# One row in four of the expert sum moved from TensorE to ScalarE and GpSimd, and the front of the work order rearranged

## Chip, cores, metric

The kernel runs on one core of a Trainium2 chip. The metric is the device time of one execution in microseconds, the median of several runs. One execution is recorded by the hardware profiler; its span and the rows below come from that one.

## What is computed

Two layers over 256 tokens of width 1024, in float32. Each layer has a mixing part and an expert part. The mixing part (RMS norm, one input projection, three kinds of attention, an S5 state space model, one output projection) is added to x. The expert part takes 128 expert rows for each token out of a table of 16384 and adds their weighted sum:

```python
q = (xc @ wq).reshape(c, PEER_HEADS, 2, PEER_QDIM // 2)
sc = jnp.einsum('thpd,hpkd->thpk', q, keys)
top_v, top_i = lax.top_k(sc, PEER_TOPK)
...
best_v, best_pos = lax.top_k(cand, PEER_TOPK)
ids = jnp.take_along_axis(cand_id, best_pos, axis=-1)
gate = jax.nn.softmax(best_v, axis=-1)
act = jax.nn.gelu(jnp.einsum('td,thkd->thk', xc, u_tab[ids])) * gate
return jnp.einsum('thk,thkd->td', act, v_tab[ids])   # added to x
```

## The kernel before

Tokens stand on the 128 partitions, so the 256 tokens are two blocks, and two layers of two blocks make four passes (PASSES, numbered 0 to 3). In each pass a token has 128 slots (SLOTS, 8 heads of 16 experts). For one slot, GpSimd issues one indirect DMA that gathers for each partition the u row and the v row of its expert, 8 KB together, 1 MB in all, into one of ten places of `ring` (RING, `ring_u` and `ring_v`). So a pass has 128 gathers and the kernel 512.

Slots are worked in groups of four (RING_G); a pass has 32 such turns (HALVES), and a turn's number in a pass is i, over the whole kernel m = 32 n + i. In a turn VectorE makes four dot products of u rows with the normed tokens (`take_dots`; the product is written back over the u row, the sum goes to `dots`), ScalarE takes their gelu (`acts`), VectorE multiplies by the gates (`weights`), and ScalarE scales the identity by each weight (`weigh`, giving `diag`). TensorE multiplies each diagonal with the v row, two halves of 512 columns, and accumulates over all 128 slots of the pass in two PSUM banks (`add_rows`, L1578). Each finished row raises `v_used`, on which GpSimd waits before it gathers into that place again, ten gathers later. At the end of a pass VectorE adds the two banks to x (`gathered`). In the last pass the tokens for the dot products are kept in PSUM, in the other passes in SBUF (`h`).

While pass n gathers, the mixing part and the search of pass n + 1 are done in between. `plan_steps` writes out one order of named steps, and each engine walks through that list and does its share of every step; inside an engine the order is fixed, between engines semaphores decide. In the list a turn is: "dots", "weigh", the search steps ("best", "pairs", "ids") and the mixing steps given to that turn, and then "rows of v". The last two turns of the last pass are done slot by slot. The mixing of pass 0 has nothing to hide behind; its order is the list `first`. The steps of it that the change touches:

- "steps 0": ScalarE's exponent of the S5 time step (L539), which waits for the load of the S5 parameters. "rows 0": TensorE transposes the tokens, VectorE and ScalarE (L599) copy four columns of blocks each into `hT`, which the projection ("columns", L1321) needs.
- "tables 0": VectorE turns sines into the S5 tables (L810 to L852); TensorE transposes its blocks in "turned 0" (L1294). "z 0": VectorE (L921) and ScalarE copy the projection out of PSUM.
- "turn back" and "turn on": VectorE's rotations before and after the S5 scan. "turn on 1" raises `s5_state`, for which TensorE's step "y 0" waits.

SyncE's queue issues all weight loads; it isn't touched. The GpSimd queue holds the gathers in order of slots.

## Time and profile before

| | us |
|---|---|
| median of 3 runs | 1610.1 |
| lowest and highest | 1606.73, 1611.24 |
| the profiled execution | 1609.26 |
| its span | 1607.4 |

The span is what the profile covers; the time of an execution has 1.9 us more around it. PE is TensorE, PEld its weight loads, DVE is VectorE, ACT ScalarE, POOL GpSimd. Each row of a group of instructions names line, engine, operation, output and inputs, and the count behind x. For TensorE one float32 multiplication shows as two instructions, so a row of v (two halves) is four. The clock that TensorE was granted stands as a share of 2.4 GHz.

### The profile page before, as it was taken

Reading aid. Unit: us, or ns where it says so; the run is one execution under the profiler, and the core shown is the slowest. Engines: PE = TensorE matmul, PEld = TensorE weight load, DVE = VectorE, ACT = ScalarE, POOL = GpSimd, SP = SyncE. Lnnn points to the kernel's source line nnn. Section 1 sums busy time; section 2 is a strip of 40 time slices with the busy share of each in tenths; the row PEclk is TensorE's granted clock in tenths of the full one; section 3 lists DMA queues with packets and bytes.
Section 4 is the critical chain, followed back from the end, with each engine's and each line's share of the span. In section 5 each row is a group of like instructions: output and inputs, shape, how many; then the busy total and the mean of one; then the engine's idle time right before and its main releaser. Section 6 shows DMA issues by size and latency. Waiting matters only on the chain.

```text
span 1607.4 us, 15416 instructions
## 1 busy us (share of the span) xinstructions
PE 1420.3 (88%) x4754; PEld 767.6 (48%) x4754; DVE 1130.7 (70%) x2797; ACT 464.6 (29%) x1127; POOL 588.5 (37%) x525
## 2 busy tenths in 40 slices
PE   6898879999998898897998799899998888877778
PEld 3667435554464344454465344555456533333333
DVE  5838998867667797785457788787556796765555
ACT  3432234342322224333121233334222222121112
POOL 1003325554323343453433434355341433434332
PEclk9999989999999999999999999999999998989999
DMA  9449999999999999999999999999999999999997
GB/s 361 153 175 381 388 377 378 402 393 420 416 412 421 410 422 363 419 420 419 421 414 402 423 422 420 421 399 396 420 418 407 374 406 423 421 421 421 421 421 328
DMA packets 103134, 632.09 MB, mean 393 GB/s; under 512 B 9697, under 2 KB 10977, under 8 KB 35214
## 3 DMA queue, kind: packets, MB, share of 16 engines
q0 software_dynamic: 74144, 537.97, 81.4%
q1 hardware_dynamic: 28910, 93.14, 14.9%
q8 instruction: 39, 0.64, 0.2%
q14 instruction: 41, 0.34, 0.1%
HBM read 630.01 MB, written 1.06 MB: 393 GB/s over the span
## 4 chain that ended last, share of the span: by engine, by line
PE 52%; DMA 20%; DVE 17%; issue 6%; ACT 3%; another core or an unknown queue 1%; POOL 0%; SPq 0%; POOLq 0%; DVEq 0%; ACTq 0%
PE ps L1578 30%; DMA ring<-table_uv,ids 20%; PE ps L1545 7%; DVE ring L1218 6%; PE ps L1358 3%; PE ps L1523 3%; PE ps L1321 2%; ACT acts L730 1%; ACT diag L753 1%; PE ps L1425 1%; PE ps L1561 1%; DVE W L996 1%; DVE W L1191 1%; DVE W L1193 1%
## 5 line engine op out<-in xcount | busy, mean ns | idle before, releaser
L1578 PE MATMUL ps<-ring,diag 128*128 128x512 f32 x2016 | 939.7, 622 | 142.7 <-ACT diag L753 129.4
L1630 POOL DMA_INDIRECT ring<-table_uv,ids x512 | 583.2, 1139 | 981.2 <-PE ps L1578 844.7
L1578 PEld LDWEIGHTS ps<-ring,diag 128*128 128x128 f32 x2016 | 394.3, 200 | 636.9 <-issue 620.4
L1218 DVE CUSTOM_DVE_ANT_0 ring<-ring,h 128x1024 f32<-128x1024 f32 x384 | 456.6, 1223 | 163.1 <-DMA ring<-table_uv,ids 160.8
L730 ACT ACTIVATE acts<-dots,small 128x4 f32<-128x4 f32 x126 | 37.4, 297 | 849.2 <-DVE dots L1218 819.8
L1218 DVE CUSTOM_DVE_ANT_0 ring<-ring,ps 128x1024 f32<-128x1024 f32 x120 | 144.7, 1220 | 95.1 <-DMA ring<-table_uv,ids 94.8
L753 ACT ACTIVATE diag<-cst,weights 128x128 f32<-128x128 f32 x504 | 161.0, 390 | 29.0 <-DVE weights L1227 28.7
L1545 PE MATMUL ps<-hT,W 128*128 128x128 f32 x960 | 114.3, 282 | 12.6 <-DMA W<-peer_wq 12.6
L1545 PEld LDWEIGHTS ps<-hT,W 128*128 128x128 f32 x960 | 113.1, 198 | 16.4 <-issue 16.4
L1358 PE MATMUL ps<-W,hT 128*128 128x512 f32 (+2 forms) x256 | 95.2, 527 | 2.7 <-DVE hT L870 2.7
L1358 PEld LDWEIGHTS ps<-W,hT 128*128 128x128 f32 x256 | 48.6, 190 | 51.9 <-issue 47.3
L1227 DVE TENSOR_TENSOR weights<-acts,gates 128x4 f32<-128x4 f32 x126 | 20.6, 163 | 53.8 <-ACT acts L730 53.8
L1523 PE MATMUL ps<-W,hT 128*128 128x512 f32 x128 | 57.3, 594 | 0.8 <-DVE hT L1084 0.8
L730 ACT ACT_TABLE_LOAD x43 | 55.2, 1283 | 4.8 <-DVE dots L1218 4.0
L1218 DVE DVE_READ_ACCUMULATOR2_ANT dots<- 128x1 f32 x504 | 41.6, 82 | 0.0
L1523 PEld LDWEIGHTS ps<-W,hT 128*128 128x128 f32 x128 | 24.0, 190 | 29.2 <-issue 28.2
L709 ACT ACTIVATE W<-ps 128x512 f32<-128x512 f32 x15 | 9.0, 597 | 97.5 <-PE ps L1545 97.5
L1019 DVE TENSOR_REDUCE small<-ps 128x4 f32<-128x512 f32 (+1 forms) x16 | 15.3, 956 | 27.1 <-PE ps L1435 14.7
L1425 PE MATMUL ps<-W 128*128 128x256 f32 (+1 forms) x128 | 31.9, 331 | 1.7 <-ACT W L661 1.7
L661 ACT ACTIVATE W<-ps,small 128x128 f32<-128x128 f32 (+1 forms) x64 | 26.0, 418 | 22.9 <-DVE small L1020 22.8
L1425 PEld LDWEIGHTS ps<-W 128*128 128x128 f32 x128 | 21.4, 191 | 7.1 <-issue 6.3
L1435 PE MATMUL ps<-bias,cst 128*128 128x128 f32 (+1 forms) x96 | 23.6, 327 | 0.0
(291 smaller groups left out, 1149.0 us busy)
## 6 DMA issues: line engine op xcount, KB each, us to landing
W<-peer_wq SPq DMA_DIRECT2D x13, 2048.0 KB, 28.5
W<-w_in SPq DMA_DIRECT2D x16, 1282.0 KB, 10.5
W<-w_out SPq DMA_DIRECT2D x8, 2048.0 KB, 18.6
ring<-table_uv,ids POOLq DMA_INDIRECT x512, 12.9
W<-w_in SPq DMA_DIRECT2D x8, 898.0 KB, 8.4
W<-w_in SPq DMA_DIRECT2D x4, 1024.0 KB, 11.5
ring<-w_in SPq DMA_DIRECT2D x2, 1544.0 KB, 18.8
ring<-w_in SPq DMA_DIRECT2D x2, 1536.0 KB, 21.1
```

The costliest lines, as they stand in the source:

```text
L661: a.activation(pbuf[:, i, 0:nk], lg[:, i * nk:(i + 1) * nk], ACT.Exp, bias=small[:, 72 + i:73 + i], accum_out=small[:, 80 + i:81 + i]).the ...
L730: a.activation(acts[:, g * RING_G:(g + 1) * RING_G], dots[:, g * RING_G:(g + 1) * RING_G], ACT.Gelu_apprx_tanh, scale=ffn_rstd[n % NB]).th ...
L753: a.activation(diag[:, s, :], ident, ACT.Copy, scale=weights[:, s:s + 1]).then_inc(diag_ready, 1)
L1218: v.tensor_tensor_reduce(ring_u[:, r, :], ring_u[:, r, :], tokens, 1.0, 0.0, ALU.mult, ALU.add, dots[:, s:s + 1]).then_inc(dots_done, 1)
L1321: mm = pe.matmul(ps[:, z_bank(0, bank), 0:c1 - c0], hT[:, k, :], first_at[group][:, k, a0:a0 + c1 - c0], start=(k == 0), stop=(k == KC - 1))
L1358: mm = pe.matmul(ps[:, 2 + i, 0:c1 - c0], hT[:, k, :], win[:, slot, c0:c1], start=(k == 0), stop=(k == KC - 1))
L1425: pe.matmul(dst, q, k, start=True, stop=False)
L1435: mm = pe.matmul(dst, flip, bias[:, t, SEQ - nk:SEQ], start=False, stop=True)
L1523: mm = pe.matmul(ps[:, 2 + c, :], hT[:, k, :], half[:, k % 4, c * 512:(c + 1) * 512], start=(k == 0), stop=(k == KC - 1))
L1545: mm = pe.matmul(ps[:, 6 + q % 2, i * P:(i + 1) * P], wq_at(n, q)[:, k, i * P:(i + 1) * P], hT[:, k, :], start=(k == 0), stop=(k == KC - 1))
L1578: mm = pe.matmul(ps[:, c, :], diag[:, s, :], ring_v[:, r, c * 512:(c + 1) * 512], start=(k == 0), stop=(k == SLOTS - 1), skip_group_check= ...
L1630: gp.indirect_dma_start(ring[:, t % RING, :], None, table_uv, bass.IndirectOffsetOnAxis(ap=ids[:, b, k:k + 1], axis=0)).then_inc(pair_in[t ...
```

## The change

In turns 0 to 28 of every pass (`added(m)`), the fourth row of v isn't multiplied by a diagonal on TensorE. ScalarE, after the turn's three diagonals, scales the row in place in `ring_v` by its weight and raises `v_scaled`. GpSimd adds it to the 1024 columns of x of this block (`add_row`), right before it issues the gather into the same place, and waits for its own add. TensorE accumulates the other rows as before; `by_pe(m)` and `adds_by[m]` count the rows of each kind, and all waits on `diag_ready` and `v_used` follow them. VectorE's `gathered` waits for the pass's adds, and its `weigh` for the scaling of two turns earlier. 116 rows take the new way, 396 the old.

In the order of pass 0, "steps 0" stands ahead of "rows 0", "tables 0" ahead of the columns and "z 0", "turn back 1" right behind "turn back 0", and "turn on 0" and "turn on 1" one entry and two entries later.

```diff
+ADD_LAST = 28
...
-    first = [["rows 0", "steps 0", "lines", "square 0", "phases 0", "sines 0", "mean 0"],
-             ["columns 0", "columns 1", "columns 2", "columns 3", "z 0", "tables 0"],
+    first = [["steps 0", "rows 0", "lines", "square 0", "phases 0", "sines 0", "mean 0", "tables 0"],
+             ["columns 0", "columns 1", "columns 2", "columns 3", "z 0"],
...
-             ["keys 0", "columns 6", "columns 7", "turn back 0", "z 1", "next square"],
-             ["logits 0", "softmax 0", "next rows", "turn back 1"],
+             ["keys 0", "columns 6", "columns 7", "turn back 0", "turn back 1", "z 1", "next square"],
+             ["logits 0", "softmax 0", "next rows"],
...
-             ["columns 9", "heads 0", "columns 10", "keys 1", "columns 11", "differ 1", "z 2", "qk sums 3", "turn on 0"],
-             ["weights 1", "logits 4", "logits 5", "next columns 0", "next columns 1", "qk scale 1", "softmax 2", "turn on 1"],
+             ["columns 9", "heads 0", "columns 10", "keys 1", "columns 11", "differ 1", "z 2", "qk sums 3"],
+             ["weights 1", "logits 4", "logits 5", "next columns 0", "next columns 1", "qk scale 1", "softmax 2", "turn on 0"],
...
-             ["heads 2", "logits 6", "co sums"],
+             ["heads 2", "turn on 1", "logits 6", "co sums"],
...
+        def added(m):
+            return m % HALVES <= ADD_LAST
...
+        def by_pe(m):
+            return RING_G * m - adds_by[m]
...
+        def own_slots(m):
+            return RING_G - added(m)
...
# ScalarE, weigh
                 if m >= 2:
-                    a.wait_ge(v_used, RING_G * (m - 1))
-                for s in range(g * RING_G, (g + 1) * RING_G):
+                    a.wait_ge(v_used, by_pe(m - 1))
+                for s in range(g * RING_G, g * RING_G + own_slots(m)):
                     a.activation(diag[:, s, :], ident, ACT.Copy, scale=weights[:, s:s + 1]).then_inc(diag_ready, 1)
+                if added(m):
+                    t = RING_G * m + RING_G - 1
+                    s, r = t % HELD, t % RING
+                    a.wait_ge(pair_in[r], 16 * (t // RING + 1))
+                    a.activation(ring_v[:, r, :], ring_v[:, r, :], ACT.Copy, scale=weights[:, s:s + 1]).then_inc(v_scaled, 1)
...
# VectorE, weigh and gathered
                 if m >= 2:
-                    v.wait_ge(diag_ready, RING_G * (m - 1))
+                    v.wait_ge(diag_ready, by_pe(m - 1))
+                    v.wait_ge(v_scaled, adds_by[m - 1])
...
             def gathered(n, i):
                 b = n % NB
+                v.wait_ge(x_added, adds_by[HALVES * (n + 1)])
...
# TensorE, add_rows
-                for j in range(RING_G):
+                for j in range(own_slots(m)):
...
-                    pe.wait_ge(diag_ready, RING_G * m + j + 1)
+                    pe.wait_ge(diag_ready, by_pe(m) + j + 1)
...
# GpSimd
+            def add_row(m):
+                t = RING_G * m + RING_G - 1
+                r, b = t % RING, m // HALVES % NB
+                gp.wait_ge(v_scaled, adds_by[m + 1])
+                if adds_by[m]:
+                    gp.wait_ge(x_added, adds_by[m])
+                gp.tensor_tensor(x[:, b, :], x[:, b, :], ring_v[:, r, :], ALU.add).then_inc(x_added, 1)
+                gp.wait_ge(x_added, adds_by[m + 1])
...
                         if t >= RING:
-                            gp.wait_ge(v_used, t - RING + 1)
+                            m, j = (t - RING) // RING_G, (t - RING) % RING_G
+                            if j < own_slots(m):
+                                gp.wait_ge(v_used, by_pe(m) + j + 1)
+                            else:
+                                add_row(m)
```

## Rows read from the trace of the kernel before

**Rows 1.** Busy time of each engine, the page

```profile
PE 1420.3 (88%) x4754; PEld 767.6 (48%) x4754; DVE 1130.7 (70%) x2797; ACT 464.6 (29%) x1127; POOL 588.5 (37%) x525
```

**Rows 2.** The costliest groups of instructions, the page

```profile
L1578 PE MATMUL ps<-ring,diag 128*128 128x512 f32 x2016 | 939.7, 622 | 142.7 <-ACT diag L753 129.4
L1630 POOL DMA_INDIRECT ring<-table_uv,ids x512 | 583.2, 1139 | 981.2 <-PE ps L1578 844.7
...
L1218 DVE CUSTOM_DVE_ANT_0 ring<-ring,h 128x1024 f32<-128x1024 f32 x384 | 456.6, 1223 | 163.1 <-DMA ring<-table_uv,ids 160.8
...
L753 ACT ACTIVATE diag<-cst,weights 128x128 f32<-128x128 f32 x504 | 161.0, 390 | 29.0 <-DVE weights L1227 28.7
```

**Rows 3.** Windows by stage: busy of each engine, PE clock, DMA share, GB/s

```profile
160.00:260.00 100.00, 85.64 (x222) 41.15 (x223) 94.06 (x268) 32.79 (x72) 34.49 (x29) 0.91 0.94 372
...
310.00:340.00 30.00, 28.44 (x105) 16.48 (x104) 24.63 (x42) 13.31 (x33) 15.38 (x11) 1.00 0.95 372
...
550.00:620.00 70.00, 69.35 (x182) 33.57 (x181) 64.63 (x171) 26.11 (x54) 27.16 (x21) 1.00 0.95 384
...
1080.00:1100.00 20.00, 18.44 (x76) 11.24 (x75) 18.63 (x33) 9.52 (x21) 10.98 (x8) 1.00 0.94 349
...
1240.00:1280.00 40.00, 39.04 (x175) 24.30 (x174) 28.03 (x90) 8.69 (x20) 15.24 (x15) 1.00 0.94 365
1280.00:1320.00 40.00, 30.63 (x63) 12.63 (x62) 37.56 (x108) 10.10 (x24) 15.47 (x16) 0.91 1.00 408
1320.00:1580.00 260.00, 205.48 (x420) 85.10 (x419) 154.26 (x310) 46.70 (x136) 98.09 (x106) 0.91 1.01 421
```

**Rows 4.** POOL's issues by source: 900 to 1260 us, then 1340 to 1580

```profile
L1630 POOL DMA_INDIRECT ring<-table_uv,ids x123: 932/942/2009, 899.7 to 1258.6; - x123
...
DMA to landing us min/median/max: 5.5/12.9/21.0
...
L1630 POOL DMA_INDIRECT ring<-table_uv,ids x95: 932/936/1287, 1346.4 to 1579.9; - x95
```

**Rows 5.** Timeline of POOL: start, duration, instruction, idle before it

```profile
226.56 0.94 POOL L1630 DMA_INDIRECT ring<-table_uv,ids  x1 [1.01 <-PE ps L1578]
...
240.98 1.87 POOL L1630 DMA_INDIRECT ring<-table_uv,ids  x1 [12.10 <-PE ps L1578]
...
245.46 0.94 POOL L1630 DMA_INDIRECT ring<-table_uv,ids  x1 [0.30 <-issue]
...
255.62 0.94 POOL L1630 DMA_INDIRECT ring<-table_uv,ids  x1 [0.47 <-PE ps L1578]
```

**Rows 6.** Timeline of DVE in the same stretch

```profile
228.82 0.19 DVE L1195 SCALAR_TENSOR_TENSOR W<-W 128x32 f32<-128x32 f32 x1
...
240.89 1.16 DVE L1218 CUSTOM_DVE_ANT_0 ring<-ring,h 128x1024 f32<-128x1024 f32 x1
...
246.41 0.42 DVE L969 TENSOR_TENSOR h<-h,small 128x256 f32<-128x256 f32 x1
...
256.96 1.22 DVE L987 TENSOR_TENSOR W<-s5t,ps 128x1024 f32<-128x1024 f32 x1
```

**Rows 7.** A square of 1024 columns on ACT, ns min/median/max

```profile
L573 ACT ACTIVATE h<-x x4: 1039/1060/1072, 12.4 to 928.8; 128x1024 f32<-128x1024 f32 x4
```

**Rows 8.** Timeline of all engines at the front

```profile
8.21 1.28 ACT L599 ACT_TABLE_LOAD   x1 [8.21 <-PE ps L1280]
...
9.51 1.14 ACT L599 ACTIVATE hT<-ps,cst 128x128 f32<-128x128 f32 x4
...
11.79 0.21 ACT L539 ACTIVATE small<-W 128x8 f32<-128x8 f32 x1 [1.15 <-DMA W<-s_in]
...
21.86 1.06 ACT L553 ACTIVATE s5t<-W 128x1024 f32<-128x1024 f32 x1
...
27.00 0.75 DVE L921 TENSOR_SCALAR h<-ps,small 128x512 f32<-128x512 f32 x1 [6.01 <-PE ps L1321]
...
36.50 1.12 PE L1294 MATMUL ps<-cst,W 128*128 128x128 f32 x4 [5.94 <-DVE W L852]
```

More of the change, by code:

```diff
@@ L345, in trunk @@
             sem("dots_done"), sem("gelu_done"), sem("weights_done"), sem("diag_ready"), sem("v_used"))
-        x_done, low_done, x_low = sem("x_done"), sem("low_done"), sem("x_low")
+        x_done, low_done, x_low, x_added = sem("x_done"), sem("low_done"), sem("x_low"), sem("x_added")
+        v_scaled = sem("v_scaled")
         dve_step, act_step = sem("dve_step"), sem("act_step")
@@ L413, in searched @@
             return {4: 1, 5: 2, 1: 3, 2: 4, 3: 5}[i] if n == 0 else 4 * n + i + 2
+        def added(m):
+            return m % HALVES <= ADD_LAST
+        adds_by = [0]
+        for m in range(HALVES * PASSES):
+            adds_by.append(adds_by[-1] + added(m))
+        def by_pe(m):
+            return RING_G * m - adds_by[m]
+        def own_slots(m):
+            return RING_G - added(m)
         def parts_done(m):
@@ L741, in weigh_one @@
                 a.wait_ge(weights_done, parts_done(m - 1) + k % RING_G + 1)
-                a.wait_ge(v_used, SLOTS * n + k + 1 - HELD)
+                a.wait_ge(v_used, by_pe(m - 2) + k % RING_G + 1)
                 a.activation(diag[:, s, :], ident, ACT.Copy, scale=weights[:, s:s + 1]).then_inc(diag_ready, 1)
@@ L1239, in weigh_one @@
                 v.wait_ge(gelu_done, parts_done(m - 1) + k % RING_G + 1)
-                v.wait_ge(diag_ready, SLOTS * n + k + 1 - HELD)
+                v.wait_ge(diag_ready, by_pe(m - 2) + k % RING_G + 1)
                 v.tensor_tensor(weights[:, s:s + 1], acts[:, s:s + 1], gates[:, n % NB, k:k + 1], ALU.mult).then_inc(weights_done, 1)
@@ L1247, in gathered @@
                     v.tensor_tensor(x[:, b, 0:512], x[:, b, 0:512], ps[:, 0, :], ALU.add).then_inc(x_low, 1)
-                    v.wait_ge(v_used, SLOTS * (n + 1))
+                    v.wait_ge(v_used, by_pe(HALVES * (n + 1)))
                     v.tensor_tensor(x[:, b, 512:D], x[:, b, 512:D], ps[:, 1, :], ALU.add).then_inc(x_done, 1)
                     return
-                v.wait_ge(v_used, SLOTS * (n + 1))
+                v.wait_ge(v_used, by_pe(HALVES * (n + 1)))
                 v.tensor_tensor(x[:, b, :], x[:, b, :], ps[:, 0:2, :].rearrange("p c n -> p (c n)"), ALU.add).then_inc(x_done, 1)
@@ L1586, in add_row @@
                 pe.wait_ge(pair_in[r], 16 * (t // RING + 1))
-                pe.wait_ge(diag_ready, t + 1)
+                pe.wait_ge(diag_ready, by_pe(t // RING_G) + k % RING_G + 1)
                 for c in range(2):
```

## The prediction

> **What bounds the kernel now.** I read the page's busy shares first [rows 1]: PE 88%, DVE 70%, POOL 37%, ACT 29%. PE looks like the bound, and the change takes work from PE. But the windows by stage [rows 3] say otherwise. From 1320 to 1580 us, where only gathered rows are consumed, the DMA engines move 421 GB/s with a share of 1.01, while PE is busy 205 of 260 us. That is the ceiling, and a gather of 1 MB (128 rows of 8 KB) costs 2.5 us of it (1.05/421). Long stretches elsewhere stand at the same rate, so relief of PE is worth something only in stretches below it. What each lost against 421 GB/s is its length times (1 - rate/421):
>
> - 160 to 260 us: 372 GB/s, 11.6 us lost, DVE 94% busy, PE 86%.
> - 310 to 340: 372, 3.5 us lost, DVE 82%, PE 95%.
> - 550 to 620: 384, 6.2 us lost, DVE 92%, PE 99%.
> - 1080 to 1100: 349, 3.4 us lost, DVE 93%, PE 92%.
> - 1240 to 1280: 365, 5.3 us lost, DVE 70%, PE 98%.
> - 1280 to 1320: 408, 1.2 us lost, DVE 94%, PE 77%.
>
> So four stretches wait at least partly for PE, 18.4 us together, and two wait for DVE, the engine that does the top-k search and the dot products. The landing time of a gather (median 12.9 us [rows 4]) against 2.5 us each says that some five are outstanding: a slot that comes free a few us late costs nothing where the rate is 421.
>
> **What the change does to PE.** A row of v costs PE 939.7/504 = 1.86 us [rows 2]. Turns 0 to 28 of four passes are 116 rows: 116 x 1.86 = 216 us of PE time go, 1.86 us per turn. Busy 1420 becomes about 1204 (75%). By the table this is cover elsewhere; it can give back at most the 18.4 us.
>
> **ScalarE.** A diagonal of 0.39 us [rows 2] becomes a scaling of 1024 columns, 1.06 us by the square of the same shape [rows 7]: +0.67 us x 116 = 78 us on an engine 29% busy. It stands after the three diagonals that PE wants, so PE's rows don't wait for it; ScalarE's next step does, by 0.67 us, which the DVE work hides (if that cover were gone: 116 x 0.67 = 78 us spread over the turns; I keep 0). It is finished 3 x 0.39 + 1.06 = 2.2 us after the weights, sooner than PE frees its third row.
>
> **GpSimd.** The trace has no POOL arithmetic. The nearest rows: DVE does a two-input pass of 128x1024 in 1.22 us [rows 2], so below 1.2 us is not to be expected; twice that, 2.4 us, is the upper bound I use (two operands read in turn). I take 2.4, the dearer end, because in this trace POOL is the engine that is slowed beside DVE: its issue of a gather takes 0.94 us at the median but up to 2.01 us where the dot products read two operands from SBUF, and at most 1.29 us in the last pass, where one operand comes from PSUM [rows 4]. POOL: 588 + 116 x 2.4 = 867 us, 54% of the span. Behind each add stand, in POOL's queue, the gather that reuses this slot and all later ones. Per turn that is 4 x 1.14 + 2.4 + about 0.2 for the wait on the add's own semaphore = 7.2 us, under the 10.1 us that DMA needs for four gathers: 0 where five are outstanding. The cover is the queue of outstanding gathers [rows 4]; if only one gather were outstanding, each turn would cost the 2.6 us.
>
> **What the add does to DVE.** This decides. Two-operand DVE passes hold up POOL's issue: the one at 240.98 took 1.87 us beside the dot products from 240.89 on, the one at 245.46, as they ended, 0.94 us [rows 5, 6]. The add reads two SBUF operands itself and is longer, so the hold can go the other way too. I lay it behind the third gather of a turn, in four turns of the trace, and ask what DVE wants then [rows 5, 6]. Where dot products are running as it comes, as at 240.89, it gets in between two of them and holds 2.4 us. After 226.56+0.94 = 227.5: the pass then running ends at 228.1, the add lasts to 230.5, and the two-input step of 228.82 waits 1.7 us. After 245.46+0.94 = 246.4: one scaling of 0.42 us is under way, then the next is held about 2.0 us. After 255.62+0.94 = 256.6: DVE reads PSUM until 259.3, nothing is held. Mean 1.5 us per add; bounds 0 (no hold) and 2.4 (always the whole).
>
> On holds the Trainium skill ("SBUF — State Buffer", section "Who interferes with whom") says that a DVE instruction with two SBUF inputs and a GpSimd one that reads SBUF exclude each other, the later one waiting for the whole of the earlier; that would put this term toward the rival of full holds below, and the stretched issues of [rows 4, 5] agree in direction. The Trainium skill ("GPSIMD Engine Reference", section 3.1) gives 4497 ns for an add of 2048 columns; half, 2.25 us, is an estimate by that page and would make the hold 1.4 us instead of 1.5.
>
> Now stage by stage. 160 to 260 us: about 7 turns with an add, 7 x 1.5 = 10.5 us; DVE is idle 5.9 us there, of which I let 1.5 absorb: +9. 550 to 620: 5 turns, 7.5 us, against 5.4 us of DVE idle: +2, and PE's 5 x 1.86 = 9.3 us buys nothing since DVE becomes the bound. 1280 to 1320: dot products read PSUM, only the search contends: +1. 1240 to 1280: DVE has room, PE saves 1.86 us in each of three or four turns: -4 of the 5.3. 310 to 340 and 1080 to 1100: DVE 82% and 93%, so PE's relief is shared with DVE's holds: -2.5 of the 6.9. Elsewhere DMA is at or near its ceiling: 0.
>
> **The front.** Two moves of consequence. First, ScalarE's exponent for the S5 state now stands before its four copies of hT. Its input landed just before 11.79 us, after the copies of before were done (table load at 8.21, copies from 9.51 for 1.14 us) [rows 8]. So table load, exponent and copies follow one another from 11.8: 1.28 + 0.21 + 1.14, and PE's first columns start at about 14.5 instead of right behind 10.65: +3.8 us. Second, the S5 tables on DVE now stand before the evacuation of z, which waited for PE until 27.00. The tables followed it, and PE, which needs them for the transposes of the blocks, stood idle 5.94 us until 36.50 [rows 8]. From 27.75 (27.00 + 0.75) that is 8.7 us of tables. They now begin when the sines are there, which was 21.86 + 1.06 = 22.9 before and is some 1.2 us later behind the moved table load, about 24.1, and end about 32.8. The evacuation follows until 33.5, the transposes of the blocks are no longer stalled behind the tables, and PE reaches the next columns about 3 us sooner in spite of its late start. The S5 rotation ("turn on"), some 8 us of DVE, and half of "turn back" only change place; the rotation now ends later against its reader (y), so part of the 3 us is lost again. Between 0 and -3, with the first bound +3.8 if the late start is not hidden: I take -1.5. SP's queue issues nothing more and nothing later. The other waits added are free: on the scaling of two turns before, and, at a pass's end, on adds that stand in POOL's queue before the last three gathers of that pass.
>
> **Sum.** +9 +2 +1 -4 -2.5 -1.5 = +4 us on the profiled execution of 1609.26 us (span 1607.4): 1613 us. The median of the runs shown is 1610.1, so that is +0.2%. 0.3% (4.8 us) is about what a measurement of this kernel can tell from no change.
>
> **Rivals.**
> - *The adds don't hold DVE* (chance 0.34). For it: no DVE row in the trace is stretched by POOL, the dot products stay at 1.22 us; against it: POOL's instructions there are short and read hardly anything. Then the DVE-bound stretches cost 0, PE's relief recovers about 12 of 18.4 us: 1609.3 - 12 - 1.5 = 1596 us.
> - *Every add holds DVE whole* (0.24). 7 x 2.4 = 17 us in 160 to 260, 5 x 2.4 - 5.4 = 7 in 550 to 620, 3 in 1280 to 1320, only 4 recovered and 1.5 at the front: +22, 1631 us. For it: from the stretched issues, whoever comes second waits. It decides from a mean hold of about 2 us; below 1.3 the whole is no slower than before.
> - *The front's late start isn't hidden* (0.06): 3.8 instead of -1.5, 1618 us. Against it speaks PE's idle 5.94 us.
> - *Forecast* (0.36), its own range 1604 to 1621: faster 0.05, same 0.21, slower 0.10.
>
> Faster: 0.34 + 0.05 = 0.39. Same: 0.21 + 0.01 from the front's rival = 0.22. Slower: 0.10 + 0.24 + 0.05 = 0.39. The range 1592 to 1631 takes in the two main rivals' values and leaves out the first's far end and the second's.
>
> **What would show it.** PE busy near 1200 us; ScalarE +78 us. The POOL add: 2.4 us, if nearer 1.3 the hold shrinks and I am too high. DVE passes with two SBUF inputs stretched to 2 to 3.6 us or gaps before them, in passes 0 to 2, none in the last pass. 160 to 260: fewer than 372 GB/s, the search ending 9 us later; the 365 GB/s at 1240 gone. PE's first columns at 14.5 us and the first gather 1.5 us earlier. Wrong would be: DVE untouched beside the adds, a rate at 550 to 620 near 421, or gathers in the 421 GB/s stretches landing so late that the rate drops there, which would make it far slower than the range.

## The result, and the profile after

The changed kernel takes 1659.8 us in the median of 4 runs (1658.65 to 1660.16), the kernel before beside it 1610.7 us. The ratio is 1.0317, with an interval of 1.0304 to 1.0331: 49 us slower, outside the predicted range and above the dearest rival (1631).

The page of the kernel after: its span, the busy time of each engine, and the engines' shares of the chain that ended last.

```profile
span 1658.4 us, 14608 instructions
...
PE 1294.9 (78%) x4290; PEld 704.1 (42%) x4290; DVE 1331.9 (80%) x2797; ACT 549.3 (33%) x1127; POOL 876.9 (53%) x641
...
DVE 40%; PE 25%; DMA 17%; issue 9%; ACT 5%; POOL 3%; another core or an unknown queue 1%; SPq 0%; DVEq 0%; POOLq 0%; ACTq 0%
```

PE has lost 125 us and is at 78%. DVE has gained 201 us with the same 2797 instructions as before: 1331.9 against 1130.7 [rows 1]. DVE is now first in the chain with 40%. In the kernel before it was PE:

```profile
PE 52%; DMA 20%; DVE 17%; issue 6%; ACT 3%; another core or an unknown queue 1%; POOL 0%; SPq 0%; POOLq 0%; DVEq 0%; ACTq 0%
```

The costliest groups (busy us, mean ns of one, idle before it and what ended it):

```profile
L1603 PE MATMUL ps<-ring,diag 128*128 128x512 f32 x1552 | 808.6, 678 | 302.8 <-ACT diag L771 292.9
...
L1241 DVE CUSTOM_DVE_ANT_0 ring<-ring,h 128x1024 f32<-128x1024 f32 x384 | 510.5, 1371 | 88.0 <-DMA ring<-table_uv,ids 85.8
...
L1634 POOL TENSOR_TENSOR x<-x,ring 128x1024 f32<-128x1024 f32 x116 | 277.2, 2390 | 2.4
...
L1251 DVE TENSOR_TENSOR weights<-acts,gates 128x4 f32<-128x4 f32 x126 | 144.3, 1145 | 54.7 <-ACT acts L748 54.7
```

The same small product in the kernel before:

```profile
L1227 DVE TENSOR_TENSOR weights<-acts,gates 128x4 f32<-128x4 f32 x126 | 20.6, 163 | 53.8 <-ACT acts L730 53.8
```

The add lasts 2.39 us. The dot products went from 1223 to 1371 ns [rows 2], 54 us in all. The last row is the larger find: the product of gelu values and gates, 128x4 elements, went from 0.163 to 1.145 us at the mean. That is 126 x 0.98 = 124 us, more than half of what DVE gained, in an instruction that had only 20.6 us before. In the trace 56 of the 126 products are long, and each of these ends within 0.05 us after an add.

Stages of [rows 3] in the kernel after (busy us of PE, PEld, DVE, ACT, POOL; PE clock, DMA share, GB/s). The same times hold somewhat earlier work here, since everything is late by 10 to 55 us.

```profile
160.00:260.00 100.00, 70.94 (x170) 33.38 (x170) 94.26 (x247) 32.79 (x60) 40.83 (x30) 0.81 0.83 322
310.00:340.00 30.00, 26.71 (x114) 17.67 (x112) 28.96 (x41) 12.84 (x31) 21.38 (x15) 0.98 0.95 353
550.00:620.00 70.00, 56.30 (x138) 26.76 (x137) 60.86 (x141) 21.05 (x39) 30.83 (x23) 0.90 0.96 398
...
1240.00:1280.00 40.00, 32.03 (x180) 23.07 (x180) 28.51 (x74) 14.35 (x30) 24.81 (x17) 0.97 1.02 413
...
1320.00:1580.00 260.00, 173.44 (x314) 71.07 (x315) 190.63 (x406) 68.46 (x140) 152.87 (x125) 0.82 1.01 414
```

160 to 260 us moves 322 GB/s instead of 372, with DVE as full as before: the same engine does less for its time. In the last pass DVE rises from 154 to 191 us and the rate is 414, not 421. Two stretches that ran at the ceiling before, before and after:

```profile
620.00:740.00 120.00, 103.89 (x364) 56.64 (x363) 88.78 (x179) 45.67 (x120) 53.74 (x46) 0.96 1.02 418
1100.00:1240.00 140.00, 131.17 (x487) 75.38 (x486) 80.34 (x193) 35.02 (x91) 55.42 (x48) 0.96 1.02 417
```

```profile
620.00:740.00 120.00, 84.43 (x270) 44.63 (x269) 113.35 (x195) 50.61 (x111) 73.44 (x50) 0.88 0.96 381
1100.00:1240.00 140.00, 120.32 (x384) 64.68 (x382) 110.58 (x163) 54.69 (x114) 97.95 (x64) 0.92 0.97 388
```

DVE goes there from 74% to 94% and from 57% to 79%, and the rate falls to 381 and 388. The page's median time from a gather's issue to its landing falls from 12.9 to 10.3 us: with gathers also issued at a slower pace, fewer of them are outstanding at a time.

The best measure of where it was lost is the time at which GpSimd issues gather number k, taken from its timeline in each kernel (us; each column after the first is the difference from before):

| gather | before | after | adds only in turns 0 to 19 | adds only in turns 20 to 28 | row scaled, not added | VectorE multiplies and adds |
|---|---|---|---|---|---|---|
| 0 | 124.0 | -2.8 | +1.9 | -1.6 | +2.1 | -2.8 |
| 32 | 226.6 | +9.8 | +21.3 | +3.3 | +6.5 | +9.5 |
| 80 | 359.6 | +20.6 | +34.1 | +5.3 | +1.0 | +7.0 |
| 160 | 614.6 | +22.5 | +34.1 | +2.5 | -1.5 | +9.9 |
| 208 | 740.5 | +38.7 | +50.2 | +2.6 | +5.0 | +13.4 |
| 256 | 893.5 | +31.3 | +49.7 | -1.0 | +0.3 | +7.9 |
| 336 | 1124.4 | +49.4 | +61.4 | +2.0 | -2.7 | +9.5 |
| 384 | 1271.3 | +46.2 | +63.0 | -1.5 | -3.3 | +9.3 |
| 464 | 1467.8 | +55.5 | +73.2 | +0.3 | +1.1 | +13.9 |
| 511 | 1586.4 | +52.6 | +69.6 | +3.8 | +1.1 | +13.5 |

A pass is 128 gathers. The kernel after loses in the first 80 gathers of each pass; behind them nothing more is lost in pass 0 and some comes back in the others: -2.8 at the first gather, then +12.6, +10.8, +1.9, +16.2, -7.4, +18.1, -3.2, +9.3, -2.9.

Each column is a single execution, so small differences say little. Three kernels that work as the kernel before does up to gather 32, but for the order of the front or the engine that makes the weights, also lose 4.8 us between gathers 0 and 32, so about 5 of the 12.6 us belong to the one trace of the kernel before. The column of turns 0 to 19 is the longest of that kernel's four runs (1678.8 us, median 1671.3).

**How a hold looks.** One turn of the first pass in the timeline of all engines (start, duration, instruction, idle before it):

```profile
171.35 1.97 POOL L1669 DMA_INDIRECT ring<-table_uv,ids  x1 [0.32 <-issue]
...
172.55 0.30 ACT L748 ACTIVATE acts<-dots,small 128x4 f32<-128x4 f32 x1 [7.54 <-DVE dots L1241]
172.88 2.84 DVE L1251 TENSOR_TENSOR weights<-acts,gates 128x4 f32<-128x4 f32 x1 [0.36 <-ACT acts L748]
173.34 2.34 POOL L1634 TENSOR_TENSOR x<-x,ring 128x1024 f32<-128x1024 f32 x1
...
175.75 0.98 ACT L771 ACTIVATE diag<-cst,weights 128x128 f32<-128x128 f32 x3 [2.90 <-DVE weights L1251]
176.30 7.99 PE L1603 MATMUL ps<-ring,diag 128*128 128x512 f32 x12 [5.73 <-ACT diag L771]
...
180.32 0.94 POOL L1669 DMA_INDIRECT ring<-table_uv,ids  x1 [3.42 <-PE ps L1603]
```

The product that should take 0.16 us is on DVE from 172.88 to 175.72. A gather's issue was under way as it came (until 173.32); the add follows at 173.34 and ends at 175.68, and only then does the product finish. ScalarE has idled 2.90 us for it, PE 5.73 us, and the gather that wants the first freed slot is issued at 180.32. The next two timelines show the other forms, a dot product in the second pass and the search in the last:

```profile
564.42 2.37 POOL L1634 TENSOR_TENSOR x<-x,ring 128x1024 f32<-128x1024 f32 x1
564.78 3.10 DVE L1241 CUSTOM_DVE_ANT_0 ring<-ring,h 128x1024 f32<-128x1024 f32 x1
...
567.81 1.21 DVE L1241 CUSTOM_DVE_ANT_0 ring<-ring,h 128x1024 f32<-128x1024 f32 x1
```

```profile
1442.19 3.47 DVE L1179 TENSOR_TENSOR W<-W 128x256 f32<-128x256 f32 x2
...
1443.01 2.36 POOL L1634 TENSOR_TENSOR x<-x,ring 128x1024 f32<-128x1024 f32 x1
...
1450.03 1.22 DVE L1241 CUSTOM_DVE_ANT_0 ring<-ring,ps 128x1024 f32<-128x1024 f32 x1
1450.33 2.36 POOL L1634 TENSOR_TENSOR x<-x,ring 128x1024 f32<-128x1024 f32 x1
```

At 564.78 a dot product comes 0.36 us behind the add and lasts 3.10 us, ending about 1.1 us after the add does; the next takes 1.21. In the last pass the two 128x256 products of the search, 0.41 us each elsewhere, last 3.47 us, while the dot product of 1450.03, whose second operand is in PSUM, keeps its 1.22 us although an add starts 0.3 us into it.

**The front.** The timeline of all engines:

```profile
11.72 0.21 ACT L557 ACTIVATE small<-W 128x8 f32<-128x8 f32 x1 [9.69 <-DMA W<-s_in]
11.83 1.12 ACT L617 ACTIVATE hT<-ps,cst 128x128 f32<-128x128 f32 x4
...
13.06 16.28 PE L1346 MATMUL ps<-W,hT 128*128 128x512 f32 x32 [4.11 <-ACT hT L617]
...
32.61 0.60 PE L1319 MATMUL ps<-cst,W 128*128 128x128 f32 x4
```

The exponent waited 9.69 us for its input, the copies followed at 11.83, and PE's first columns began at 13.06. The transposes of the blocks stand at 32.61 us, against 36.50 before [rows 8], and the next columns followed at 33.04, 4.4 us sooner than before (37.41), where about 3 had been forecast.

### The profile page after: what moved, and what is told of

The parts are those of the page before. It is cut to its first block, busy times and chain, and to the rows that moved or that the text cites. A ratio compares the mean times of both kernels' runs of the same rounds, so it can differ in the third digit from the quotient of the medians.

```text
span 1658.4 us, 14608 instructions
## 1 busy us (share of the span) xinstructions
PE 1294.9 (78%) x4290; PEld 704.1 (42%) x4290; DVE 1331.9 (80%) x2797; ACT 549.3 (33%) x1127; POOL 876.9 (53%) x641
## 4 chain that ended last, share of the span: by engine, by line
DVE 40%; PE 25%; DMA 17%; issue 9%; ACT 5%; POOL 3%; another core or an unknown queue 1%; SPq 0%; DVEq 0%; POOLq 0%; ACTq 0%
DMA ring<-table_uv,ids 15%; DVE ring L1241 14%; PE ps L1603 14%; DVE weights L1251 7%; PE ps L1570 6%; DMA W<-peer_wq 2%; POOL ring L1669 2%; ACT acts L748 1%; DVE W L1216 1%; DVE W L1214 1%; DVE W L1217 1%; PE ps L1548 1%; DVE W L1019 1%; POOL x L1634 1%
## 5 line engine op out<-in xcount | busy, mean ns | idle before, releaser
L1603 PE MATMUL ps<-ring,diag 128*128 128x512 f32 x1552 | 808.6, 678 | 302.8 <-ACT diag L771 292.9
L1669 POOL DMA_INDIRECT ring<-table_uv,ids x512 | 594.3, 1161 | 742.2 <-PE ps L1603 573.2
L1603 PEld LDWEIGHTS ps<-ring,diag 128*128 128x128 f32 x1552 | 329.8, 219 | 734.5 <-issue 721.6
L1241 DVE CUSTOM_DVE_ANT_0 ring<-ring,h 128x1024 f32<-128x1024 f32 x384 | 510.5, 1371 | 88.0 <-DMA ring<-table_uv,ids 85.8
L1634 POOL TENSOR_TENSOR x<-x,ring 128x1024 f32<-128x1024 f32 x116 | 277.2, 2390 | 2.4
L1251 DVE TENSOR_TENSOR weights<-acts,gates 128x4 f32<-128x4 f32 x126 | 144.3, 1145 | 54.7 <-ACT acts L748 54.7
L771 ACT ACTIVATE diag<-cst,weights 128x128 f32<-128x128 f32 x388 | 127.1, 391 | 152.7 <-DVE weights L1251 152.7
L776 ACT ACTIVATE ring<-ring,weights 128x1024 f32<-128x1024 f32 x116 | 131.4, 1133 | 0.0
L1216 DVE TENSOR_TENSOR W<-W 128x512 f32<-128x512 f32 (+1 forms) x34 | 26.9, 792 | 1.2
## 6 DMA issues: line engine op xcount, KB each, us to landing
ring<-table_uv,ids POOLq DMA_INDIRECT x512, 10.3
```

What stands on the lines that cost most here:

```text
L771: a.activation(diag[:, s, :], ident, ACT.Copy, scale=weights[:, s:s + 1]).then_inc(diag_ready, 1)
L776: a.activation(ring_v[:, r, :], ring_v[:, r, :], ACT.Copy, scale=weights[:, s:s + 1]).then_inc(v_scaled, 1)
L1216: step(v.tensor_tensor(hits, hits, bc(i4[:, :, s, :], 2, TOPK), ALU.mult))
L1241: v.tensor_tensor_reduce(ring_u[:, r, :], ring_u[:, r, :], tokens, 1.0, 0.0, ALU.mult, ALU.add, dots[:, s:s + 1]).then_inc(dots_done, 1)
L1251: v.tensor_tensor(weights[:, ss], acts[:, ss], gates[:, b, i * RING_G:(i + 1) * RING_G], ALU.mult)\
L1603: mm = pe.matmul(ps[:, c, :], diag[:, s, :], ring_v[:, r, c * 512:(c + 1) * 512], start=(k == 0), stop=(k == SLOTS - 1), skip_group_check= ...
```

## The experiments

**The two halves of the change.** One kernel has only the new order of the front:

```diff
-    first = [["rows 0", "steps 0", ... "mean 0"],
-             ["columns 0", ... "z 0", "tables 0"],
+    first = [["steps 0", "rows 0", ... "mean 0", "tables 0"],
+             ["columns 0", ... "z 0"],
```

> The kernel before with only the new order of the front. In the changed kernel the first gather was issued at 121.3 us instead of 124.0. Theory H (the adds hold VectorE) says the order is not what costs: first gather again near 121.3, time 2 to 3 us below before (0.998 to 0.999). The rival that the order does the harm (the S5 rotation too late for its reader, ScalarE late) wants a good part of the 49 us here: 1.01 or more.

1.0003 [0.9988, 1.0017]. Nothing that can be measured, where 2 to 3 us had been expected. Its first gather goes out at 125.6 us against 124.0; over the seventeen kernels profiled here that time scatters from 120.2 to 126.4, with either order, so the 4 us seen at 33 us cannot be found again at the gathers. The other kernel is the change with the old order:

> The changed kernel with the front order of before. Theory H: all of the loss stays and the front's gain goes, 1660 + 2.8 = about 1663 us (1.032 to 1.035 of before), first gather near 124. If the order and the adds do harm together: clearly under 1650.

1.0346 [1.0323, 1.0368], DVE busy 1335.6 us. The whole loss is the adds'.

**What the relief is worth by itself.** The row is neither multiplied nor added, so that its part of the sum is left out:

```diff
-                    a.activation(ring_v[:, r, :], ring_v[:, r, :], ACT.Copy, scale=weights[:, s:s + 1])
+                    a.activation(ring_v[:, r, 0:1], ring_v[:, r, 0:1], ACT.Copy, scale=weights[:, s:s + 1])
...
-                gp.tensor_tensor(x[:, b, :], x[:, b, :], ring_v[:, r, :], ALU.add).then_inc(x_added, 1)
```

> The fourth row of turns 0 to 28 is not used at all: no product on PE, no scaling (ScalarE scales a single column), no add; its gather and its dot product stay. This is the whole relief of PE with no cost beside it, left out of the sum. Theory H with the DMA ceiling: only the stretches below 421 GB/s that wait for PE come back, 8 to 18 us, plus 2.8 us of the front: 1590 to 1600. If PE were the bound of the kernel, up to 216 us of PE time would show in the end: under 1560.

0.9946 [0.9928, 0.9965]: 8.7 us, less than expected (1606.6 us, not 1590 to 1600). Its page:

```profile
PE 1288.1 (80%) x4290; PEld 704.0 (44%) x4290; DVE 1132.2 (71%) x2797; ACT 451.1 (28%) x1127; POOL 581.8 (36%) x525
```

PE is as relieved as in the kernel after (1288 against 1295 us), DVE is where it was before. So 116 of 512 rows taken from PE for nothing, nearly a quarter, bring half a per cent. With ScalarE's scaling of the whole row and still no add:

```diff
-                if adds_by[m]:
-                    gp.wait_ge(x_added, adds_by[m])
-                gp.tensor_tensor(x[:, b, :], x[:, b, :], ring_v[:, r, :], ALU.add).then_inc(x_added, 1)
-                gp.wait_ge(x_added, adds_by[m + 1])
```

> ScalarE scales the fourth row, GpSimd does nothing with it (left out of the sum) and only waits for the scaling. Between the run with the row left out (0.9946) and that with GpSimd's write of zeros (1.0002) this says whose the 9 us are: near 0.995 if the occupied GpSimd queue (1.8 us per add) cost them, near 1.000 if ScalarE's 1.13 us did. I expect the first, 0.995 to 0.998, since ScalarE's scaling stands behind the diagonals.

0.9956 [0.9940, 0.9971]. The 99 us of ScalarE time cost 0.0010, 1.6 us, which is within the uncertainty of the two ratios.

**Is it the reading of SBUF?** The add is replaced by a GpSimd instruction that only writes (the row is left out of the sum):

```diff
-                gp.tensor_tensor(x[:, b, :], x[:, b, :], ring_v[:, r, :], ALU.add).then_inc(x_added, 1)
+                gp.memset(ring[:, r, :], 0.0).then_inc(x_added, 1)
```

> GpSimd's add is replaced by a write of zeros over the same place of the ring, 2048 columns, which reads nothing from SBUF; the fourth rows of turns 0 to 28 are left out of the sum. GpSimd's queue is still occupied before the same gathers for about 1 to 2.4 us, ScalarE still scales, PE is relieved. Theory H (reads of the add exclude VectorE's passes with two SBUF inputs): VectorE's weights product back at 0.16 us from 1.15, dot products 1.22 from 1.37, time at or under before, 1595 to 1610. Rival Q (the add delays the gathers in GpSimd's queue): time stays near 1660 minus what the write is shorter, so 1640 or more.

1.0002 [0.9989, 1.0015], 1614 us, a little above the 1595 to 1610 expected and far from the rival's 1640. From the page of this kernel:

```profile
L1241 DVE CUSTOM_DVE_ANT_0 ring<-ring,h 128x1024 f32<-128x1024 f32 x384 | 457.8, 1226 | 198.2 <-DMA ring<-table_uv,ids 192.6
...
L1634 POOL MEMSET ring<- 128x2048 f32 x116 | 211.1, 1820 | 0.1
...
L1251 DVE TENSOR_TENSOR weights<-acts,gates 128x4 f32<-128x4 f32 x126 | 20.8, 165 | 48.4 <-ACT acts L748 47.7
```

116 writes of 1.82 us run beside DVE, and both DVE rows stand where they stood before: 1226 and 165 ns. These writes are 0.57 us shorter than the adds. With a second write of 640 columns behind the first:

```diff
+                gp.memset(ring[:, r, :], 0.0).then_inc(half_written, 1)
+                gp.wait_ge(half_written, adds_by[m + 1])
+                gp.memset(ring[:, r, 0:640], 0.0).then_inc(x_added, 1)
```

> As the run with GpSimd's write of zeros, lengthened by a second write of 640 columns to about 2.6 us with the wait between, a little longer than the add's 2.39; fourth rows left out of the sum. Reads nothing, holds nothing. Run with 1.82 us: 1.0002, without it 0.9956. If the queue's cost grows with the length: 1.002 to 1.006, so that the queue has some 10 of the 60 us between the changed kernel and the row left out. If the queue were the cause of the convex rest, 1.015 or more.

1.0019 [1.0005, 1.0033].

```profile
PE 1295.2 (80%) x4290; PEld 708.5 (44%) x4290; DVE 1160.7 (72%) x2797; ACT 549.6 (34%) x1127; POOL 869.0 (54%) x757
```

GpSimd is as busy as with the adds (869 against 877 us), DVE has gained 30 us and not 201. These 30 us are holds too, but of other instructions: mostly casts and scalings, which take one tensor. The cast of search results before, and in this kernel:

```profile
L1182 DVE CAST W<-W 128x64 f32<-128x64 uint32 x15 | 3.8, 252 | 0.0
```

```profile
L1205 DVE CAST W<-W 128x64 f32<-128x64 uint32 x15 | 10.1, 675 | 0.0
```

Against the kernel that scales and doesn't add, the writes cost 1.0019 - 0.9956 = 0.0063, some 10 us; each of the two has about 0.0015 of uncertainty on either side. How much of it is the occupied queue and how much these holds was not separated.

**Less reading.** One operand read, as a copy within the ring (row left out of the sum):

```diff
+                gp.tensor_copy(ring_u[:, r, :], ring_v[:, r, :]).then_inc(x_added, 1)
```

> GpSimd copies the scaled row onto the used u row (one SBUF operand read, 1024 columns) instead of adding it to x; the fourth rows of turns 0 to 28 are left out of the sum. Theory H (any read of GpSimd excludes VectorE's two-operand passes for the time of the whole GpSimd instruction): weights product and dot products are stretched again in proportion to the copy's duration; with a copy of about half the add's 2.39 us some 20 us of the 49 come back as loss, 1625 to 1640 on the scale of 1614 before. Rival (only GpSimd instructions with two operands contend): 1614 as with the write.

1.0026 [1.0013, 1.0039], 1619.5 us: below the 1625 to 1640 expected, and above the rival's 1614. Whether the copy holds VectorE is read from the rows:

```profile
L1634 POOL COPY ring<-ring 128x1024 f32<-128x1024 f32 x116 | 126.2, 1088 | 0.8
...
L1251 DVE TENSOR_TENSOR weights<-acts,gates 128x4 f32<-128x4 f32 x126 | 60.9, 483 | 48.8 <-ACT acts L748 48.4
```

And the add on half of the columns (the other half is left out):

```diff
+                gp.tensor_tensor(x[:, b, 0:512], x[:, b, 0:512], ring_v[:, r, 0:512], ALU.add).then_inc(x_added, 1)
```

> The add over 512 of the 1024 columns; the other half of the fourth rows is left out of the sum. Theory H, dose and response: add about 1.2 us, hold per add half (VectorE's extra busy time about 90 us instead of 201), and since the first holds are taken up by slack the loss falls by more than half: 1620 to 1632 on the scale of 1614 before. Rival Q (one more instruction in GpSimd's queue with its wait, whatever its length): 1645 or more.

1.0049 [1.0034, 1.0064], 1622 us. DVE gained 90 us (1220.8).

```profile
L1634 POOL TENSOR_TENSOR x<-x,ring 128x512 f32<-128x512 f32 x116 | 153.5, 1323 | 2.4
...
L1251 DVE TENSOR_TENSOR weights<-acts,gates 128x4 f32<-128x4 f32 x126 | 74.1, 588 | 48.5 <-ACT acts L748 48.5
```

The copy of 1.09 us holds the small product to 483 ns, the add of 1.32 us to 588, the add of 2.39 us to 1145, the write of 1.82 us to 165. One reading operand is enough to hold it, and the hold grows with the length of the instruction. The price grows faster than the hold: from the free relief it is 0.0103 for 90 us on DVE and 0.0371 for 201.

**Taking the small product off DVE.** ScalarE makes the weights, with the gates as its scale; and the same in the kernel before, as the control:

```diff
+                for j in range(RING_G):
+                    s, k = g * RING_G + j, RING_G * i + j
+                    w = a.activation(weights[:, s:s + 1], acts[:, s:s + 1], ACT.Copy, scale=gates[:, n % NB, k:k + 1])
+                w.then_inc(weights_done, 1)
```

> The changed kernel, but ScalarE makes the weights: four copies of acts with the gate as scale, in place of VectorE's product of acts and gates, the instruction that was stretched most (0.16 to 1.15 us, 124 of VectorE's extra 201 us). Theory H with the weights as the place that counts: the add runs beside instructions that matter less, 1625 to 1645 on the scale of 1614 before. If it doesn't matter which instruction is held because VectorE is full: the hold moves to the dot products and the time stays at 1655 or more.

> The kernel before with ScalarE making the weights, no adds: the control of the run above. It takes two crossings between engines and 0.16 us of VectorE out of each turn and adds about 0.8 us of ScalarE. With the DMA ceiling at 421 GB/s I expect no more than 5 us either way, 0.997 to 1.003.

1.0232 [1.0203, 1.0261] with the adds (1650 us, between the two expectations), 1.0037 [1.0023, 1.0051] without, just above the range expected. The page with the adds, and its dot products:

```profile
PE 1294.5 (79%) x4290; PEld 707.1 (43%) x4290; DVE 1250.9 (76%) x2671; ACT 656.8 (40%) x1631; POOL 880.6 (54%) x641
...
L1252 DVE CUSTOM_DVE_ANT_0 ring<-ring,h 128x1024 f32<-128x1024 f32 x384 | 525.7, 1407 | 138.9 <-DMA ring<-table_uv,ids 136.7
```

The adds now cost 1.0232 - 1.0037 = 0.0195 instead of 0.0317. So about 40% of the loss hung on the small product being on DVE. The rest moved to what DVE does instead: the dot products are at 1407 ns, and DVE is busy 140 us more than the control's 1111.

**Where in a pass.** The adds in turns 20 to 28 only (36 of them), and in 0 to 19 only (80):

```diff
-            return m % HALVES <= ADD_LAST
+            return 20 <= m % HALVES <= ADD_LAST
```

```diff
-ADD_LAST = 28
+ADD_LAST = 19
```

> Adds only in turns 20 to 28 of each pass, 36 adds, the turns that hold no mixing steps of the next pass but its queries and, early, nothing of the search of this one. By the issue times of the gathers the changed kernel lost nothing there. Theory H with a full VectorE as its condition: 0.997 to 1.002 of before. If each add costs the same wherever it stands (49/116 = 0.42 us): 36 x 0.42 = 15 us, 1.009.

> The other part: adds in turns 0 to 19, 80 adds. Theory H with its condition: the whole loss stays, 1.028 to 1.036. Same cost everywhere: 80 x 0.42 = 34 us, 1.021.

1.0000 [0.9986, 1.0014] and 1.0349 [1.0329, 1.0368].

```profile
PE 1376.3 (85%) x4610; PEld 750.3 (47%) x4610; DVE 1195.0 (74%) x2797; ACT 490.8 (30%) x1127; POOL 688.4 (43%) x561
```

```profile
PE 1350.7 (81%) x4434; PEld 733.8 (44%) x4434; DVE 1272.4 (76%) x2797; ACT 523.3 (31%) x1127; POOL 781.8 (47%) x605
```

DVE gains 64 us from 36 adds and 142 us from 80, 1.79 and 1.77 us per add: the hold is the same at both places, and its price is nothing at the one and the whole loss at the other. Turns 0 to 19 are where most of the next pass's mixing steps (normalization, S5) and the rest of the search stand between the dot products.

**The same work on DVE itself.** VectorE multiplies and adds in one instruction of 1.285 us, right behind the weights; ScalarE and GpSimd do nothing for it, and the sum is complete:

```diff
+                if added(m):
...
+                    v.scalar_tensor_tensor(out=x[:, b, :], in0=ring_v[:, r, :], scalar=weights[:, s:s + 1], in1=x[:, b, :],
+                                           op0=ALU.mult, op1=ALU.add).then_inc(x_added, 1)
```

> VectorE itself multiplies and adds the fourth row to x in one pass right behind the weights; ScalarE and GpSimd do nothing for it. The sum is complete. VectorE gets 116 x 1.22 = 142 us more of its own work, against 201 us of holds in the changed kernel, PE is relieved as there. If the end follows VectorE's busy time: between the half-width add (+90 us, 1.005) and the changed kernel (+201 us, 1.032), so 1.010 to 1.020. If what hurt was the place of the hold (the weights product, which all else in the turn waits for): below 1.008.

1.0045 [1.0027, 1.0063]. 141 us more on DVE (1272.1), as many as the 80 adds brought, for an eighth of their loss against the kernel before; counted from the free relief it is 0.0099, about a quarter of the 0.0371 of all 116 adds. Then with the long writes in GpSimd's queue as well:

> VectorE multiplies and adds (1.0045 alone), and GpSimd's queue is occupied by the same 2.6 us of writes before the gather. Sum complete. If the two costs simply add up: 1.0045 + 0.008 = 1.012. If VectorE's extra work and a later gather make each other worse, as they would have to in the changed kernel to explain its 1.032: 1.020 or more.

1.0134 [1.0110, 1.0158]: the writes cost 0.0089 here, against 0.0063 beside a less busy DVE. With 0.003 to 0.004 of uncertainty in the comparison the two are not told apart, so the costs add up as far as can be seen. And last, only the order is changed: the fourth weight alone, then the multiply-add, then the three weights that ScalarE and PE wait for:

```diff
+                    v.tensor_tensor(weights[:, s:s + 1], acts[:, s:s + 1], gates[:, b, k:k + 1], ALU.mult).then_inc(v_scaled, 1)
...
+                    v.scalar_tensor_tensor(out=x[:, b, :], in0=ring_v[:, r, :], scalar=weights[:, s:s + 1], in1=x[:, b, :],
+                                           op0=ALU.mult, op1=ALU.add).then_inc(x_added, 1)
+                    v.tensor_tensor(weights[:, s0:s0 + RING_G - 1], acts[:, s0:s0 + RING_G - 1], gates[:, b, k + 1 - RING_G:k],
+                                    ALU.mult).then_inc(weights_done, 1)
```

> VectorE makes the weight of the fourth row first, multiplies and adds that row (1.28 us), and only then makes the other three weights, on which ScalarE, PE and the freeing of the slots wait. Same work as in the run where the addition stands behind the weights (1.0045), plus 0.16 us a turn. Placement theory (a microsecond ahead of the weights is dear, behind them cheap): 1.012 to 1.025. If only VectorE's busy time counts: 1.005 to 1.008.

1.0120 [1.0097, 1.0143]. The timelines of the kernel with the multiply-add behind the weights, and ahead of them:

```profile
178.02 0.16 DVE L1245 TENSOR_TENSOR weights<-acts,gates 128x4 f32<-128x4 f32 x1 [0.36 <-ACT acts L748]
178.22 0.99 ACT L771 ACTIVATE diag<-cst,weights 128x128 f32<-128x128 f32 x3 [0.23 <-DVE weights L1245]
178.22 1.28 DVE L1253 SCALAR_TENSOR_TENSOR x<-ring,weights,x 128x1024 f32<-128x1024 f32 x1
...
178.76 8.27 PE L1605 MATMUL ps<-ring,diag 128*128 128x512 f32 x12 [4.77 <-ACT diag L771]
```

```profile
179.93 1.28 DVE L1253 SCALAR_TENSOR_TENSOR x<-ring,weights,x 128x1024 f32<-128x1024 f32 x1
181.13 0.16 DVE L1255 TENSOR_TENSOR weights<-acts,gates 128x3 f32<-128x3 f32 x1
...
181.32 0.99 ACT L771 ACTIVATE diag<-cst,weights 128x128 f32<-128x128 f32 x3 [1.62 <-DVE weights L1255]
...
181.86 7.70 PE L1610 MATMUL ps<-ring,diag 128*128 128x512 f32 x12 [5.37 <-ACT diag L771]
```

In the first, the diagonals start 0.20 us after the weights began and run beside the multiply-add. In the second they wait 1.4 us longer (1.62 against 0.23 us), and PE's rows start behind them. The same work, plus a second small product of 0.16 us a turn, costs 0.0075 (uncertain by 0.003), 12 us, more there: 0.10 us for each of 116 turns per 1.4 us of delay. That only some of the turns are short of time is the likely reason; no run shows which.

## Why the prediction was wrong

**The parts, as measured.** From the free relief (0.9946) to the kernel after (1.0317) are 0.0371, 60 us. ScalarE's scaling is 0.0010 of it and equally long writes in GpSimd's queue 0.0063, together 12 us. The remaining 0.030, 48 us, is there when GpSimd reads SBUF and gone when it only writes: two-operand work on DVE held by the adds. These are differences of ratios with about 0.002 of uncertainty each.

**What was right.** PE's relief as a thing of little worth (8.7 us by itself). The add at 2.4 us (2.39), which was the upper bound of a guess from a VectorE row, and GpSimd at 867 us (877). ScalarE +78 us (+85). The mean hold of 1.5 us was 0.2 short: 201/116 = 1.73; that is partly luck, since 62% of it fell on an instruction that the prediction did not look at. That dot products with an operand in PSUM go untouched; but "none in the last pass" was wrong, since search steps and 12 small products were held there. And the holds themselves: here the trace agrees with the Trainium skill ("SBUF — State Buffer", section "Who interferes with whom"), by which a DVE instruction with two SBUF inputs and a GpSimd one that reads SBUF exclude each other (dot products of 3.10 us beside the add, 1.22 us when one operand is in PSUM). The estimate by the Trainium skill ("GPSIMD Engine Reference", section 3.1), half of 4497 ns or 2.25 us, was 0.14 short of the measured 2.39.

**The step that failed: "Elsewhere DMA is at or near its ceiling: 0."** The forecast put a price on the holds of some 12 turns, and a shared one on a handful more, of the 116 with an add; that is why even its rival with 2.4 us for each add came only to 1631. Laid on the table of gathers, the stretches that I priced came out near their price. 160 to 260 us: +9 forecast, +12.6 by gather 32, some 5 of which are the scatter named above. 550 to 620: +2 forecast, +1.9 between gathers 80 and 160. 1240 to 1280: -4 forecast, -3.2 between 336 and 384. The stretches that I booked at nothing carry the loss: +10.8 between 32 and 80, +16.2 between 160 and 208, +18.1 between 256 and 336 (-2.5 was booked for a part of this and of the first together), +9.3 between 384 and 464 (about half of this, +4.5, also stands in the kernel with the row left out). The rates say the same: 381 instead of 418 GB/s from 620 to 740 us, 388 instead of 417 from 1100 to 1240. The ceiling of 421 GB/s was taken as a cover, as if a stretch near it had room for anything. A rate near the ceiling says that DMA is served in time by the engines as they are; it doesn't say how far they are from serving it late. With 1.73 us per turn on DVE and the rows' release behind it, they fell below. The prediction named this among what would make it wrong, and gave it no chance.

The +2 at 550 to 620 was luck. "PE's 5 x 1.86 = 9.3 us buys nothing since DVE becomes the bound" is not what the row left out shows: its rate there is 415 GB/s instead of 384, and it gains 5.9 us between gathers 128 and 160. The changed kernel loses 1.9 us there, so the holds cost near 8, where 7.5 had been counted and all but 2 written off against DVE's idle time; the relief covered the difference.

**The second step: a hold priced by its length alone.** I asked what DVE wants as the add comes, and counted dot products and search steps. The instruction that the add most often met was the weights product (56 of 116 adds): ScalarE's diagonals, PE's rows and the freeing of ring slots all stand behind it, so a hold there delays the turn itself and not only DVE's next step. It could have been seen in the trace of before: at the third gather's issue of 245.46 us [rows 5] that product follows at 245.86, and the prediction passed over it to the scaling of 246.41. The runs bear it out: without that product on DVE the adds cost 0.0195 instead of 0.0317, and DVE's own work of 141 us costs 0.010 over the free relief behind the weights and 0.017 ahead of them. In the turn shown the likely reason for the meeting is that the product comes at the end of the dot products, beside which the gather's issue ahead of the add was stretched to 1.97 us (171.35); in 33 of the 56 cases an issue was under way as the product came.

**The third: a queue cost of 0.** "0 where five are outstanding" was wrong by up to 10 us (0.0063), less what the holds of casts and scalings by the writes have of it. In the profiles the kernel with the long writes is 3.5 us ahead of the one without at the first gather (122.6 and 126.1 us), 8.0 behind at gather 80 (368.6 and 360.6) and 7.7 behind at the last (1595.2 and 1587.5). So in this pair of profiles the mean of 7.2 us per turn against 10.1 holds from then on, and the cost arises in the first 80 gathers, where in the kernel before the rate was 372 and GpSimd stood idle for PE, up to 12.10 us before a gather [rows 5]. That a gather there is not one of five outstanding that can wait is a reading, not shown by a run of its own.

**The clock was not it.** PE's matmuls went from 622 to 678 ns at a mean granted clock of 0.892 instead of 0.959, and 1204 x 0.959/0.892 = 1294 is what PE's busy time fell to (1295). But the kernel with the row left out has nearly the same (671 ns, clock 0.906) and is the fastest of all, so a clock at this level did not cost it its gain.

**The front.** The mechanism was there and earlier than forecast (columns at 13.06, not 14.5, since the table load was done while ScalarE waited), and it was worth nothing measurable instead of -1.5 us.

**What stays open.** The multiply-add ahead of the weights (0.0120), the writes in GpSimd's queue (0.0089) and the scaling (0.0010) add up to 0.022 of the 0.0317. The price rises faster than the hold (0.0103 for 90 us, 0.0371 for 201), the hold is 1.73 us against the multiply-add's 1.285, and it strikes other instructions too; whether that makes the remaining 0.010 was not separated. Nor is it settled why the adds in turns 0 to 19 alone (1.0349) cost no less than all 116 (1.0317, and 1.0346 with the old order). No version that computes the whole sum beat the kernel before: the nearest are the adds in turns 20 to 28 (1.0000) and VectorE's multiply-add (1.0045).

## What to carry to other kernels

Before work goes to GpSimd, list each VectorE instruction that reads two SBUF operands, the smallest too, and ask who waits for it: a 0.16 us product at the head of a chain costs more when it is held than a long one at its end. A stretch at the DMA ceiling is no cover by itself; it needs the slack of the chain that frees the buffers. And price the relief first: here a run with the row left out showed that all of it was worth half a per cent, less than VectorE's own multiply-add costs.

## What the runs showed of the hardware that was not expected

- A GpSimd instruction with a single SBUF operand (the copy, 1.09 us) holds VectorE's two-operand products as the add does (mean 483 ns instead of 163). One that only writes (1.82 us for 2048 columns) does not (165 ns).
- Writes hold other instructions of VectorE, with one tensor: beside the long writes the 128x64 casts took 675 ns at the mean instead of 252, and three scalings of only 128x4 took 1.78 to 2.18 us instead of 0.16, each with a write of 1.82 us under way before it ended. VectorE gained 30 us in all.
- A held instruction pays the whole wait whatever its size: a 128x4 product lasted up to 2.99 us, a dot product up to 4.05.
- A VectorE TENSOR_SCALAR of 128x128 with one SBUF tensor and a per-partition scalar was held too: two of them took 3.37 us beside an add at 580.63 us, 0.61 us in the kernel before.
- The hold can begin up to 0.6 us before the add's recorded start (the product of 172.88 us, the add of 173.34). The gather's issue under way by then doesn't explain it: in the kernel before 69 of the small products came during an issue and none lasted over 0.23 us. What does was not found.
